# Two small query blocks of the first layer's attention share one round: 16 steps of differential attention become 12

## Chip, cores and metric

One core of a Trainium2 chip runs the kernel. The metric is the device time of one execution in microseconds (us). All times below come from one profiled execution or from the timed runs.

## What is computed

Two transformer blocks in a row over 512 tokens of width 1024, batch 1. The change lies in the attention of the very first layer: 4 heads of differential attention, each with two score maps of head width 64 and values of width 128, in query blocks of 128 with causal key prefixes:

```python
s = jnp.einsum('bqhmd,bkhmd->bhmqk', qi, kf) * scale + bias      # m = 0, 1; bias: ALiBi, causal
p = jax.nn.softmax(s, axis=-1)
attn = p[:, :, 0] - lam * p[:, :, 1]
return jnp.einsum('bhqk,bkhe->bqhe', attn, vf)                   # then an RMS norm per head
```

Beside it in the same layer stands a pooling mixer of 4 groups, and both results go through an output projection. Then come a convolutional gated feed-forward part, a sliding-window layer with its own feed-forward part, and the second block.

## The kernel before

**Weights.** Every large product is made in float32 accuracy from halves: `hi` (ScalarE rounds the loaded weights `raw` to `w_hi`), `lo` (VectorE subtracts, `w_lo = raw - w_hi`), and three products of 512 columns each (hi*hi, hi*lo, lo*hi). Weights come in slabs of 2048 columns through two alternating halves of `raw`, `w_hi` and `w_lo`. Slab s may be rounded once slab s-2 is used up, and used once its `lo` is complete (`lo_done`).

**Stage A.** Slabs 0 to 4 are plain. Slabs 5 to 7 (`A_MORE`, 144 products) and the first two slabs of the output projection, 8 and 9 (`A_OUT`, 96 products), are woven in small portions between the steps of the attention, so that TensorE has work while the softmax goes over the other engines. `A_FILL` cuts these 240 products into portions, one for each step. Products form units that end in one PSUM bank: 24 products for a unit of slabs 5 to 7, 12 for one of slabs 8 and 9. Units take turns in two banks, so that one begins only when the unit before the last has been read (`unit_read`).

**Step g** of the attention, before the change, is head g // 4 and query block g % 4 (key width 128, 256, 384 or 512). Each engine has its own hand-written queue, in program order:

- TensorE: `scores(g)` (2 matmuls, banks 4 and 5), `fill(g)` (a portion of `A_FILL`), `turn(g-1)` (transposes of the finished probabilities into bank 6), then jobs of other chains (`norm_job`: sums of squares for the norms of q and k; `pool_product`; `turn_v`: transposes of a head's values; `squares_summed`: sums of squares over a head's output), then `values(g-2)`.
- VectorE: `finish(g-1)` (reciprocal of the row sums, scaling, difference of the two maps), `maxima(g)` (bias, negation and row minimum), then `scaled`, `output`, `pooled_low`, `sub_scale`, the reading of finished units (`evacuate`), `lo_piece` (the `lo` of a slab, of slabs 8 and later in two halves one step apart), `alibi`, `pool_group`.
- ScalarE: norms and copies of the other chains, `exps(g)`, `copy(g-1)` (the transposed probabilities to SBUF), `hi_piece` (the `hi` of the slab after one that begins in this step).
- GpSimd, in one order over the heads: squares of q and k; then for each of heads 0 to 2 the square of its output (after `output`) and the `lo` half of its normed output (after ScalarE's `sub_split`).
- SyncE: one load for each slab, slab s behind `lo_done` of slab s-2.

Of the kernel before, what the change touches and what calls it, by code (L numbers as in the profile page):

```python
# [112 lines left out]
X_ROUNDS = [(0, 1), (2,), (3,)]  # L113
X_STEPS = 8 * len(X_ROUNDS)
# [48 lines left out]
def blocks_program(nc, weights, xt, params, consts, scratch, out):  # L163
    with ExitStack() as ctx:
# [183 lines left out]
        def f_blocks(r):  # L348

            out, col = [], 0  # L350
            for i in X_ROUNDS[r % 3]:
                out.append((i, col, (i + 1) * P))
                col += (i + 1) * P
            return out

        def f_width(r):
            return sum(w for _, _, w in f_blocks(r))

        def f_done(r):

            return 2 * (4 * (r // 3) + (0, 2, 3)[r % 3])
# [52 lines left out]

        def a_width(g):
            return (g % 4 + 1) * P
# [292 lines left out]
        def _(pe):  # L709
# [106 lines left out]
            def a_stage():  # L816
# [54 lines left out]
                def scores(g):  # L871
                    it, i = g // 4, g % 4
                    if i == 0:
                        pe.wait_ge(d_qk, 2 * it + 2)
                    if g:
                        pe.wait_ge(d_max, 2 * g)
                    for m in range(2):
                        h = 64 * m
                        pe.matmul(psum[:, 4 + m, 0:a_width(g)], qn[it % 2][h:h + 64, i * P:(i + 1) * P], kn[it % 2][h:h + 64, 0:a_width(g)],  # L879
                                  start=True, stop=True).then_inc(d_scored, 1)  # L880

                def turn(g):
                    pe.wait_ge(d_fin, g + 1)
                    if g:
                        pe.wait_ge(d_copied, g)
                    for j in range(g % 4 + 1):
                        last = pe.transpose(psum[:, 6, j * P:(j + 1) * P], a_prob(0, g)[:, j * P:(j + 1) * P], ident)
                    last.then_inc(d_pt, 1)

                def values(g):  # L890
                    it, i = g // 4, g % 4
                    if i == 0:
# [3 lines left out]
                    pe.wait_ge(d_copied, g + 1)  # L896
                    for j in range(i + 1):
                        last = pe.matmul(psum[:, 0, i * P:(i + 1) * P], vtok[it % 2][:, j * P:(j + 1) * P],
                                         a_slot(g)[:, j * P:(j + 1) * P],
                                         start=(i == 0), stop=(i == 3 and j == 3), skip_group_check=True)  # L900
                    last.then_inc(d_pv, 1)
# [25 lines left out]
                for g in range(A_STEPS + 2):  # L927
                    it = g // 4
                    if g < A_STEPS:
                        scores(g)  # L930
                    fill(g)
                    if 1 <= g <= A_STEPS:
                        turn(g - 1)
                    if g % 4 < 2 and it + 1 < A_HEADS:
                        norm_job(2 * (it + 1) + g % 4, 1)
                    if g in (2, 3, 5, 6):
                        pool_product((2, 3, 5, 6).index(g))
                    if g == 1:
                        turn_v(1)
                    elif g in (9, 10):  # L940
                        turn_v(g - 7)
                    elif g % 4 == 3 and it:
                        squares_summed(it - 1)
                    if g >= 2:
                        values(g - 2)
                fill(A_STEPS + 2)
                squares_summed(A_HEADS - 1)
                fill(A_STEPS + 3)
# [145 lines left out]
            def x_stage():  # L1094
                so, xo = FIRST["S_OUT"], FIRST["X_OUT"]

                def mask(r):

                    if r:
                        pe.wait_ge(f_max, f_done(r))  # L1100
                    for m in range(2):
                        for i, col, w in f_blocks(r):
# [3 lines left out]
                def scores(r):  # L1106
# [3 lines left out]
                    for i, col, w in f_blocks(r):  # L1110
                        for m in range(2):
# [3 lines left out]
                            if i == X_ROUNDS[r % 3][-1]:  # L1115
                                last.then_inc(f_scored, 1)

                def turn(r):
                    for m in range(2):
# [3 lines left out]
                        for j in range(f_width(r) // P):  # L1123
# [3 lines left out]
                def values(r):  # L1127
# [6 lines left out]
                    for i, col, w in f_blocks(r):  # L1134
# [201 lines left out]
        def _(act):  # L1336
# [101 lines left out]
            def a_stage():  # L1438
# [15 lines left out]
                def v_copy(it):  # L1454

                    act.wait_ge(d_turned_v, it + 1)
                    if it >= 2:
                        act.wait_ge(d_pv, 4 * (it - 1))
# [27 lines left out]
                def exps(g):  # L1486
                    w = a_width(g)
                    for m in range(2):
                        n = 2 * (g % 4) + m
                        act.wait_ge(d_max, 2 * g + m + 1)  # L1490
                        pr = a_prob(m, g)[:, 0:w]
                        act.activation(pr, pr, ACT.Exp, scale=-1.0, bias=neg_max[:, n:n + 1],
                                       accum_out=row_sum[:, n:n + 1]).then_inc(d_exp, 1)

                def copy(g):
                    w = a_width(g)
                    act.wait_ge(d_pt, g + 1)
                    if g >= 2:
                        act.wait_ge(d_pv, g - 1)
                    act.activation(a_slot(g)[:, 0:w], psum[:, 6, 0:w], ACT.Identity).then_inc(d_copied, 1)  # L1500
# [12 lines left out]
                for g in range(A_STEPS + 2):  # L1513
                    it = g // 4
                    if g % 4 in (1, 2) and it + 1 < A_HEADS:
                        norm_job(2 * (it + 1) + g % 4 - 1, 1)
                    if g in (3, 4, 6, 7):
                        pooled_high((3, 4, 6, 7).index(g))
                    if g == 2:
                        v_copy(1)  # L1520
                    elif g in (10, 11):
                        v_copy(g - 8)
                    elif g % 4 == 0 and it >= 2:
                        sub_norm(it - 2)
                    elif g % 4 == 1 and it >= 2:
                        sub_split(it - 2)
                    if g < A_STEPS:
                        exps(g)
                    if 1 <= g <= A_STEPS:
                        copy(g - 1)  # L1530
                    for s in A_FILL[1][g]:
                        hi_piece(s + 1, 0, 1)
                act.wait_ge(d_pv, A_STEPS)
# [228 lines left out]
            def x_stage():  # L1762
                so, xo = FIRST["S_OUT"], FIRST["X_OUT"]

                def exps(r):
                    n = f_done(r)
                    for m in range(2):
                        for i, col, w in f_blocks(r):
# [6 lines left out]
                def copy(r):  # L1775
                    w = f_width(r)
# [80 lines left out]
        def _(dve):  # L1857
# [93 lines left out]
            def a_stage():  # L1951
# [45 lines left out]
                def maxima(g):  # L1997
                    it, w = g // 4, a_width(g)
                    if g % 4 == 0:
                        me.wait()  # L2000
                    if g >= 2:
                        dve.wait_ge(d_pt, g - 1)
                    for m in range(2):
                        n = 2 * (g % 4) + m
                        dve.wait_ge(d_scored, 2 * g + m + 1)
                        dve.tensor_tensor_reduce(
# [788 lines left out]
```

## Time and profile before

| | us |
|---|---|
| Median of 3 runs | 1901.89 (1901.38 to 1901.93) |
| The profiled execution | 1901.86 |
| Its span, first to last instruction | 1900.0 |
| TensorE busy (share of the span) | 1881.6 (99%) |
| VectorE busy | 1176.5 (62%) |
| ScalarE busy | 789.6 (42%) |
| GpSimd busy | 138.5 (7%) |

The table is read against the 1.9 us by which the execution is longer than its span. The busy shares are those of the whole program; the attention of stage A runs from about 68 to 161 us of it.

### The profile page before, as it was taken

Reading aid. Unit: us, or ns where it says so; the run is one execution under the profiler, and the core shown is the slowest. Engines: PE = TensorE matmul, PEld = TensorE weight load, DVE = VectorE, ACT = ScalarE, POOL = GpSimd, SP = SyncE. Lnnn points to the kernel's source line nnn. Section 1 sums busy time; section 2 is a strip of 40 time slices with the busy share of each in tenths; the row PEclk is TensorE's granted clock in tenths of the full one; section 3 lists DMA queues with packets and bytes.
Section 4 is the critical chain, followed back from the end, with each engine's and each line's share of the span. In section 5 each row is a group of like instructions: output and inputs, shape, how many; then the busy total and the mean of one; then the engine's idle time right before and its main releaser. Section 6 shows DMA issues by size and latency. Waiting matters only on the chain.

```text
span 1900.0 us, 24418 instructions
## 1 busy us (share of the span) xinstructions
PE 1881.6 (99%) x9034; PEld 1504.0 (79%) x9034; DVE 1176.5 (62%) x1826; ACT 789.6 (42%) x1184; POOL 138.5 (7%) x102
## 2 busy tenths in 40 slices
PE   8999999999999999999999999999999999999999
PEld 6767888888887788888888887878777788888887
DVE  5786677356646866763566498665656666744762
ACT  4365443133435654432334343422566544322441
POOL 2012100000021110000000101111211020000000
PEclk9999999999999999999999999999999999999999
DMA  6112222322231122223232322444433122233222
GB/s 216 67 58 72 93 88 88 111 89 102 71 106 65 46 89 89 88 88 111 89 102 76 121 89 91 144 149 156 134 128 112 49 96 100 77 100 111 89 78 99
DMA packets 38304, 186.51 MB, mean 98 GB/s; under 512 B 4384, under 2 KB 4768, under 8 KB 23376
## 3 DMA queue, kind: packets, MB, share of 16 engines
q1 hardware_dynamic: 37936, 185.22, 28.8%
q8 instruction: 49, 0.80, 0.2%
q10 hardware_dynamic: 288, 0.23, 0.0%
q14 instruction: 31, 0.25, 0.0%
HBM read 176.95 MB, written 8.49 MB: 98 GB/s over the span
## 4 chain that ended last, share of the span: by engine, by line
PE 92%; DVE 5%; ACT 2%; DMA 1%; issue 1%; SPq 0%; DVEq 0%; ACTq 0%
PE banks L723 55%; PE banks L1199 22%; PE banks L773 4%; PE banks L1113 1%; PE banks L1138 1%; DVE w_lo L1869 1%; PE banks L1124 1%; PE banks L1272 1%; PE banks L1243 1%; PE banks L1084 1%; DVE tmp L2255 1%; PE banks L1255 1%; PE banks L1212 1%; ACT w_hi L1352 1%; DMA raw<-weights 1%; PE banks L879 1%
## 5 line engine op out<-in xcount | busy, mean ns | idle before, releaser
L723 PE MATMUL banks<-xn_hi,w_hi 128*128 128x512 f32 x1240 | 486.5, 392 | 6.4 <-DVE w_lo L2632 6.4
L723 PE MATMUL banks<-xn_hi,w_lo 128*128 128x512 f32 x1240 | 483.6, 390 | 0.0
L723 PE MATMUL banks<-xn_lo,w_hi 128*128 128x512 f32 x1240 | 478.1, 390 | 0.0
L1352 ACT ACTIVATE w_hi<-raw 128x2048 fp32r<-128x2048 f32 (+2 forms) x134 | 228.3, 1704 | 230.6 <-PE banks L723 194.2
L1869 DVE TENSOR_TENSOR w_lo<-raw,w_hi 128x2048 fp32r<-128x2048 f32 (+2 forms) x134 | 274.9, 2051 | 46.0 <-ACT w_hi L1352 45.6
L723 PEld LDWEIGHTS banks<-xn_hi,w_hi 128*128 128x128 f32 x1240 | 233.6, 188 | 57.6 <-DMA con<-consts 6.3
L723 PEld LDWEIGHTS banks<-xn_lo,w_hi 128*128 128x128 f32 x1240 | 233.4, 188 | 49.5 <-issue 1.4
L723 PEld LDWEIGHTS banks<-xn_hi,w_lo 128*128 128x128 f32 x1240 | 233.5, 188 | 48.6
L1414 ACT ACTIVATE tmp<-scaled_h,par 128x512 f32<-128x512 f32 x132 | 100.6, 809 | 349.2 <-DVE scaled_h L1914 349.1
L1914 DVE TENSOR_TENSOR scaled_h<-banks,token_rs 128x512 f32<-128x512 f32 x132 | 85.1, 686 | 184.9 <-PE banks L723 164.7
L1199 PE MATMUL banks<-xn_hi,w_hi 128*128 128x512 f32 x408 | 165.6, 406 | 1.0 <-DVE big L1964 0.6
L1199 PE MATMUL banks<-xn_lo,w_hi 128*128 128x512 f32 x408 | 162.4, 398 | 0.0
L1199 PE MATMUL banks<-xn_hi,w_lo 128*128 128x512 f32 x408 | 162.1, 397 | 0.0
L723 PE MATMUL banks<-hid_hi,w_hi 128*128 128x512 f32 x396 | 154.0, 389 | 0.0
L723 PE MATMUL banks<-hid_lo,w_hi 128*128 128x512 f32 x396 | 154.0, 389 | 0.0
L723 PE MATMUL banks<-hid_hi,w_lo 128*128 128x512 f32 x396 | 154.0, 389 | 0.0
L1887 DVE TENSOR_TENSOR x<-banks,x 128x512 f32<-128x512 f32 (+1 forms) x48 | 33.2, 692 | 178.4 <-PE banks L723 157.2
L638 POOL TENSOR_TENSOR sq<-sq 128x512 f32<-128x512 f32 x38 | 59.2, 1558 | 858.0 <-ACT sq L1358 837.4
L1922 DVE SCALAR_TENSOR_TENSOR tmp<-scaled_h,par,tmp 128x511 f32<-128x511 f32 x132 | 98.8, 748 | 34.9 <-ACT tmp L1414 34.9
L1926 DVE SCALAR_TENSOR_TENSOR tmp<-scaled_h,par,tmp 128x510 f32<-128x510 f32 x132 | 99.1, 750 | 15.1 <-DVE tmp L1922 13.0
L2122 DVE TENSOR_TENSOR w_lo<-raw,w_hi 128x1024 fp32r<-128x1024 f32 (+1 forms) x61 | 82.4, 1355 | 40.6 <-ACT w_hi L1554 40.6
L1199 PEld LDWEIGHTS banks<-xn_hi,w_hi 128*128 128x128 f32 x408 | 76.6, 188 | 30.6 <-issue 13.1
(270 smaller groups left out, 2564.3 us busy)
## 6 DMA issues: line engine op xcount, KB each, us to landing
raw<-weights SPq DMA_DIRECT2D x116, 1024.0 KB, 4.9
raw<-weights SPq DMA_DIRECT2D x24, 768.0 KB, 4.3
raw<-weights SPq DMA_DIRECT2D x24, 640.0 KB, 3.9
big<-scratch SPq DMA_DIRECT2D x40, 256.0 KB, 4.6
att<-scratch SPq DMA_DIRECT2D x16, 256.0 KB, 4.6
scratch<-stage SPq DMA_DIRECT2D x12, 256.0 KB, 4.3
scratch<-con SPq DMA_DIRECT2D x12, 256.0 KB, 2.0
out<-x SPq DMA_DIRECT2D x4, 512.0 KB, 4.0
```

Source lines behind the costliest of these rows:

```text
L638: pool.tensor_tensor(chunk(sq, 0), chunk(sq, 0), chunk(sq, c), ALU.add).then_inc(sq_summed, 1)
L723: return pe.matmul(psum[:, 2 * p + m, :], w[:, at_:at_ + P], x_part(k), start=start, stop=stop)
L773: return pe.matmul(psum[:, 2 * (s % 2), :], w[:, at_:at_ + P], x_part(k), start=(k == 0 and t == 0), stop=(k == k_n - 1 and t == 2))
L1199: ins = pe.matmul(c_bank(u), w[:, at_:at_ + P], x_part(k), start=(k == 0 and t == 0), stop=(k == k_n - 1 and t == 2))
L1352: act.activation(w_hi[:, sl], raw[:, sl], ACT.Identity).then_inc(hi_done, 1)
L1414: act.activation(chunk(tmp, 2 * j + m), chunk(scaled_h, 2 * j + m), ACT.Identity, bias=pcol(conv_b, c), scale=pcol(conv, 3 * c + 2)).then_ ...
L1869: dve.tensor_tensor(w_lo[:, sl], raw[:, sl], w_hi[:, sl].bitcast(F32), ALU.subtract).then_inc(lo_done, 1)
L1887: last = dve.tensor_tensor(chunk(x, c), psum[:, 2 * ((a + j) % 2) + m, :], chunk(x, c), ALU.add)
L1914: dve.tensor_tensor(chunk(scaled_h, 2 * j + m), psum[:, 2 * ((a + j) % 2) + m, :], token_rs[:, :], ALU.mult).then_inc(h_scaled, 1)
L1922: me.mark(dve.scalar_tensor_tensor(out=chunk(tmp, t, 1), in0=bank[:, 0:T - 1], scalar=pcol(conv, 3 * c + 1), in1=chunk(tmp, t, 1), op0=ALU ...
L1926: dve.scalar_tensor_tensor(out=chunk(tmp, t, 2), in0=bank[:, 0:T - 2], scalar=pcol(conv, 3 * c), in1=chunk(tmp, t, 2), op0=ALU.mult, op1=A ...
L2122: ins = dve.tensor_tensor(w_lo[:, sl], raw[:, sl], w_hi[:, sl].bitcast(F32), ALU.subtract)
```

## The change

Query blocks 0 and 1 of a head share a round: their scores lie side by side in the two score banks (128 and 256 columns of 512), and so do their transposes in bank 6. Blocks 2 and 3 have a round each. A head has three rounds instead of four steps, all heads 12 instead of 16. All matmuls, transposes, exponentials, minima and scalings stay as many and as wide as they were. Only the reciprocal, the copy of the transposes and the waits go by round.

The 240 woven products are cut anew, and the jobs of the other chains get new places in the order. The functions that name the blocks of a round exist already for the second block's attention; they get neutral names and serve both.

```diff
-A_STEPS = 4 * A_HEADS
-A_FILL = weave([("A_MORE", 3), ("A_OUT", 2)], [20] * 4 + [16] + [12] * 4 + [7] * 8 + [8] + [12, 20])
+BLOCK_ROUNDS = [(0, 1), (2,), (3,)]
+A_ROUNDS = len(BLOCK_ROUNDS) * A_HEADS
+A_FILL = weave([("A_MORE", 3), ("A_OUT", 2)], [24] * 6 + [12] * 3 + [8, 8, 4] + [4, 4] + [12, 20])
...
+                    for i, col, w in round_blocks(r):
+                        for m in range(2):
+                            h = 64 * m
+                            last = pe.matmul(psum[:, 4 + m, col:col + w], qn[it % 2][h:h + 64, i * P:(i + 1) * P], kn[it % 2][h:h + 64, 0:w],
+                                             start=(col == 0), stop=True, skip_group_check=True)
+                            if i == BLOCK_ROUNDS[r % 3][-1]:
+                                last.then_inc(d_scored, 1)
...
+                for r in range(A_ROUNDS + 2):
+                    it = r // 3
+                    if r < A_ROUNDS:
+                        scores(r)
+                    fill(r)
+                    if 1 <= r <= A_ROUNDS:
+                        turn(r - 1)
+                    if r % 3 < 2 and it + 1 < A_HEADS:
+                        norm_job(2 * (it + 1) + r % 3, 1)
+                    if r == 0:
                         turn_v(1)
...
+                    elif r == 2:
+                        pool_product(0)
+                        pool_product(1)
+                    elif r == 3:
+                        pool_product(2)
+                    elif r == 5:
+                        pool_product(3)
+                    elif r in (7, 8):
+                        turn_v(r - 5)
+                    elif r in (6, 9, 11):
+                        squares_summed((6, 9, 11).index(r))
+                    if r >= 2:
+                        values(r - 2)
...
+                for r in range(A_ROUNDS + 2):
+                    it = r // 3
+                    if r in (7, 10, 12):
+                        sub_norm((7, 10, 12).index(r))
+                    if r in (1, 8, 9):
+                        v_copy((1, 8, 9).index(r) + 1)
+                    if r % 3 and it + 1 < A_HEADS:
+                        norm_job(2 * (it + 1) + r % 3 - 1, 1)
...
+                    if r in (8, 11, 13):
+                        sub_split((8, 11, 13).index(r))
+                    if r < A_ROUNDS:
+                        exps(r)
+                    if 1 <= r <= A_ROUNDS:
+                        copy(r - 1)
+                    for s in A_FILL[1][r]:
                         hi_piece(s + 1, 0, 1)
...
+                for r in range(A_ROUNDS + 2):
+                    it = r // 3
+                    if 1 <= r <= A_ROUNDS:
+                        finish(r - 1)
+                    if r < A_ROUNDS:
+                        maxima(r)
+                    if r % 3 and it + 1 < A_HEADS:
+                        scaled(2 * (it + 1) + r % 3 - 1)
+                    if r % 3 == 2 and 1 <= it < A_HEADS:
                         output(it - 1)
...
+                    if r == 3:
+                        pooled_low(0)
+                        pooled_low(1)
+                    elif r in (4, 6):
+                        pooled_low(2 if r == 4 else 3)
+                    if r in (7, 10, 12):
+                        h = (7, 10, 12).index(r)
+                        sub_scale(h, chunk(big, h))
+                    if r:
+                        for s, m in A_FILL[2][r - 1]:
                             evacuate(s, m)
                     for q in range(2):
...
+                        if r > q:
+                            for s in A_FILL[1][r - q - 1]:
                                 if s + 1 >= o:
                                     lo_piece(s + 1, q, 2)
```

Read from the list of portions: slabs 5, 6 and 7 begin in rounds 0, 2 and 4, slab 8 in round 6, slab 9 in the middle of round 10. `A_FILL[1][r]` is the list of slabs that begin in round r, `A_FILL[2][r]` that of the units that end in it. The last two portions, behind the last `values`, are 12 and 20 products as before.

## Rows read from the trace of the kernel before

**Rows 1.** The page: busy time by engine, and the chain that ended last.
```profile
PE 1881.6 (99%) x9034; PEld 1504.0 (79%) x9034; DVE 1176.5 (62%) x1826; ACT 789.6 (42%) x1184; POOL 138.5 (7%) x102
...
PE 92%; DVE 5%; ACT 2%; DMA 1%; issue 1%; SPq 0%; DVEq 0%; ACTq 0%
```

**Rows 2.** Timeline of TensorE: start, duration, line, tiles, shape; L879 scores, L898 values.
```profile
67.83 0.49 PE L879 MATMUL banks<-att 64*128 64x128 f32 x4
...
88.11 0.38 PE L898 MATMUL banks<-att 128*128 128x128 f32 x2
88.43 1.13 PE L879 MATMUL banks<-att 64*128 64x512 f32 x4
...
95.48 0.61 PE L898 MATMUL banks<-att 128*128 128x128 f32 x4
96.02 0.49 PE L879 MATMUL banks<-att 64*128 64x128 f32 x4
...
101.50 0.83 PE L898 MATMUL banks<-att 128*128 128x128 f32 x6
102.26 0.70 PE L879 MATMUL banks<-att 64*128 64x256 f32 x4
102.89 0.50 PE L1199 MATMUL banks<-xn_hi,w_hi 128*128 128x512 f32 x1
```

**Rows 3.** Windows, each from a portion's first product to the next piece's start.
```profile
68.25:72.92 4.67, 4.67 (x23) 3.87 (x22) 4.50 (x13) 2.69 (x5) 0.00 (x0) 1.00 0.00 0
125.24:126.97 1.73, 1.73 (x9) 1.38 (x8) 1.52 (x5) 1.73 (x6) 0.91 (x1) 1.00 0.01 5
133.97:136.59 2.62, 1.89 (x9) 1.23 (x8) 2.51 (x7) 0.00 (x0) 0.00 (x0) 1.00 0.00 0
138.79:141.19 2.40, 1.90 (x10) 1.24 (x8) 2.29 (x6) 1.50 (x3) 0.00 (x0) 1.00 0.39 58
150.15:152.81 2.66, 1.96 (x9) 1.31 (x8) 2.29 (x7) 1.52 (x4) 0.00 (x0) 1.00 0.00 0
157.10:159.41 2.31, 2.20 (x12) 1.51 (x11) 2.31 (x4) 0.94 (x2) 0.95 (x1) 1.00 0.00 0
160.21:163.35 3.14, 3.13 (x15) 2.27 (x14) 2.74 (x3) 0.60 (x1) 0.37 (x1) 1.00 0.28 42
```

**Rows 4.** Timeline of TensorE: a wait before a product of step 2.
```profile
84.20 0.47 PE L1199 MATMUL banks<-xn_hi,w_hi 128*128 128x512 f32 x1 [0.56 <-DVE big L1964]
```

**Rows 5.** Timeline of VectorE: L2006 minima, L2030 pooled_low, L1964 unit read, L2122 lo.
```profile
89.70 0.69 DVE L2006 CUSTOM_DVE_ANT_0 att<-banks,att 128x512 f32<-128x512 f32 x1 [3.48 <-PE banks L879]
...
96.68 0.29 DVE L2006 CUSTOM_DVE_ANT_0 att<-banks,att 128x128 f32<-128x128 f32 x1 [0.58 <-PE banks L879]
...
116.87 0.75 DVE L2030 SCALAR_TENSOR_TENSOR big_r<-banks,par,big_r 128x512 fp32r<-128x512 f32 x1
117.54 0.68 DVE L1964 TENSOR_TENSOR big<-banks,token_rs 128x512 f32<-128x512 f32 x1
118.14 1.22 DVE L2122 TENSOR_TENSOR w_lo<-raw,w_hi 128x1024 fp32r<-128x1024 f32 x1
...
132.65 2.06 DVE L2122 TENSOR_TENSOR w_lo<-raw,w_hi 128x1024 fp32r<-128x1024 f32 x1
```

**Rows 6.** Timeline of ScalarE: hi of a slab, and sub_split.
```profile
153.73 1.90 ACT L1554 ACTIVATE w_hi<-raw 128x2048 fp32r<-128x2048 f32 x1
...
157.75 0.63 ACT L1484 ACTIVATE big_r<-big 128x512 fp32r<-128x512 f32 x1 [0.33 <-DVE big L2036]
```

**Rows 7.** Timeline of GpSimd: L659 lo of a head's output, L657 its square.
```profile
126.06 1.29 POOL L659 TENSOR_TENSOR big_r<-big,big_r 128x512 fp32r<-128x512 f32 x1 [13.23 <-ACT big_r L1484]
132.15 1.48 POOL L657 TENSOR_TENSOR tn<-big 128x512 f32<-128x512 f32 x1 [4.80 <-DVE big L2025]
...
148.68 1.04 POOL L657 TENSOR_TENSOR tn<-big 128x512 f32<-128x512 f32 x1 [4.05 <-DVE big L2025]
```

**Rows 8.** A window at the start of the kernel.
```profile
6.00:12.00 6.00, 5.64 (x13) 4.46 (x14) 3.62 (x7) 4.20 (x8) 0.00 (x0) 1.00 1.03 370
```

More of the change, by code:

```diff
@@ L354, in f_blocks, with round_width, blocks_done @@
             return out
-        def f_width(r):
-            return sum(w for _, _, w in f_blocks(r))
-        def f_done(r):
+        def round_width(r):
+            return sum(w for _, _, w in round_blocks(r))
+        def blocks_done(r):
             return 2 * (4 * (r // 3) + (0, 2, 3)[r % 3])
@@ L895, in values @@
                             pe.wait_ge(d_out, it)
[L896 to L900, printed above, removed]
+                    pe.wait_ge(d_copied, r + 1)
+                    for i, col, w in round_blocks(r):
+                        for j in range(i + 1):
+                            last = pe.matmul(psum[:, 0, i * P:(i + 1) * P], vtok[it % 2][:, j * P:(j + 1) * P],
+                                             a_slot(r)[:, col + j * P:col + (j + 1) * P],
+                                             start=(i == 0), stop=(i == 3 and j == 3), skip_group_check=True)
                     last.then_inc(d_pv, 1)
@@ L926, in a_stage @@
                 pe.wait_ge(banks_read, 4)
[L927 to L938, printed above, removed]
-                        turn_v(1)
[L940 to L946, printed above, removed]
+                for r in range(A_ROUNDS + 2):
[8 more added lines that the diff above has]
+                    if r == 0:
+                        turn_v(1)
+                    elif r == 2:
[11 more added lines that the diff above has]
+                        values(r - 2)
+                fill(A_ROUNDS + 2)
                 squares_summed(A_HEADS - 1)
-                fill(A_STEPS + 3)
+                fill(A_ROUNDS + 3)
                 for s in (FIRST["A_OUT"] + 2, FIRST["A_OUT"] + 3):
@@ L1109, in scores @@
                         pe.wait_ge(f_qk, 2 * it + 2)
-                    for i, col, w in f_blocks(r):
+                    for i, col, w in round_blocks(r):
                         for m in range(2):
@@ L1512, in a_stage @@
                 hi(5, 0)
[L1513 to L1531, printed above, removed]
+                for r in range(A_ROUNDS + 2):
+                    it = r // 3
+                    if r in (7, 10, 12):
[5 more added lines that the diff above has]
+                    if r == 3:
+                        pooled_high(0)
+                        pooled_high(1)
+                    elif r in (4, 6):
+                        pooled_high(2 if r == 4 else 3)
+                    if r in (8, 11, 13):
[5 more added lines that the diff above has]
+                    for s in A_FILL[1][r]:
                         hi_piece(s + 1, 0, 1)
-                act.wait_ge(d_pv, A_STEPS)
+                act.wait_ge(d_pv, A_ROUNDS)
                 act.wait_ge(sub_stat, A_HEADS - 1)
@@ L2019, in finish @@
                     me.wait()
-                    dve.scalar_tensor_tensor(out=p0, in0=p0, scalar=row_inv[:, n:n + 1], in1=p1,
-                                             op0=ALU.mult, op1=ALU.add).then_inc(d_fin, 1)
+                    for i, col, w in blocks:
+                        n = 2 * i
+                        p0, p1 = a_prob(0, r)[:, col:col + w], a_prob(1, r)[:, col:col + w]
+                        last = dve.scalar_tensor_tensor(out=p0, in0=p0, scalar=row_inv[:, n:n + 1], in1=p1, op0=ALU.mult, op1=ALU.add)
```

165 lines of the change are left out of this document (75 added, 90 removed).

## The prediction

> **What bounds the kernel now.** I read the page first. TensorE is busy 99% of the span and makes up 92% of the chain that ended last [rows 1]. So only two things can shorten this kernel: less work on TensorE, or less waiting of TensorE. What the softmax engines save by themselves is worth nothing.
>
> Then I read TensorE's timeline of the attention stage piece by piece, to get a price for each piece and to see where it stood still. A wait that is shorter than a matmul's modelled end hides in the busy time, so I take waits from start to start: a portion of 20 products takes 4.67 and one of 7 takes 1.73 [rows 3]. That makes 0.226 for a product and 0.15 for going from the scores into a portion. By this price three portions of 7 should take 1.73 and took 2.62, 2.40 and 2.66; one of 8 should take 1.96 and took 2.31; one of 12 should take 2.86 and took 3.14 [rows 3]. The waits are 0.89 + 0.67 + 0.93 + 0.35 + 0.28 = 3.1, and with the 0.56 in step 2 [rows 4] 3.7. The idle before a row counts from a modelled end, so the last one is a little more: 3.7 to 4.2, of which I take **4.0 us of waits** in the stage. Two kinds are among them: VectorE's `finish` is late for `turn` (the first two), and a unit's bank is read late (the others).
>
> The matmuls themselves stay the same in number and width, so 4.0 us plus the small cost of passing between pieces is all that the change can win: about 0.26% of the kernel.
>
> **The change part by part.**
>
> *Fewer groups on TensorE.* Four portions fewer to enter: 4 x 0.15 = 0.60. The scores of blocks 0 and 1 cost 0.42 (67.83 to 68.25) and 0.63 (102.26 to 102.89) [rows 2, 3], together 1.05 as before. `values` costs 0.32 for one matmul, 0.54 for two and 0.76 for three [rows 2]: three in one go instead of one and two save 0.10 a head, 0.40 in all. One `norm_job` now stands directly ahead of scores where two pieces did before; by the same kind of passage I put 0.1 against it. Gain: **0.9 us**, between 0.6 and 1.0.
>
> *The old waits.* In rounds 0 to 5 each portion is a whole unit of 24 products, 24 x 0.226 + 0.15 = 5.6 us, and a unit's bank has a full round to be read. The 0.56 goes. In the later rounds a `finish` is due after a longer round (8 to 12 products and the longer jobs, instead of 7), and the unit of products 192 to 203 ends two rounds ahead of the reader that needs its bank. I let all 4.0 us go; between 3.7 and 4.2 if they all do. What may stay is a term of its own below.
>
> *VectorE and ScalarE.* Four reciprocals and four copies fewer, as many minima, exponentials and scalings. Both engines are off the path, so this is nothing by itself. What counts is the order.
>
> *A new wait at round 6: the second half of slab 8's `lo`.* Slab 7 begins in round 4. So `hi` of slab 8 is made in ScalarE's round 4, and VectorE makes the first half of its `lo` in round 5 and the second half in round 6. But TensorE's portion of round 6 begins with slab 8 and waits for the whole `lo`. On VectorE that half stands behind `maxima(6)`, which needs `scores(6)`, which TensorE issues directly ahead of the portion. Counted from the start of `scores(6)`:
> - Minima can start about 1.2 later. For one block the distance was 1.27 at 512 columns (88.43 to 89.70) and 0.66 at 128 (96.02 to 96.68) [rows 2, 5]. For two blocks the first map is ready only with the third matmul, 0.42 + 0.32 after the start, plus a tail of 0.45 to 0.74 (0.66 less the 0.21, 1.27 less the 0.53 that the first matmul takes): 1.2 to 1.5.
> - Four minima, two of 128 and two of 256 columns. The rows are 0.29 and 0.69 long, of which the last 0.08 overlaps what follows [rows 5]: 0.21 at 128, 0.61 at 512, so some 0.35 at 256: 1.12.
> - `pooled_low(3)` 0.67, the reading of the unit that ended in round 5, 0.60, and the half slab, 1.22 (116.87, 117.54, 118.14) [rows 5].
>
> The sum is 1.2 + 1.12 + 0.67 + 0.60 + 1.22 = 4.8; `scores(6)` itself covers 1.05. TensorE stands for **3.8 us**. The half slab took 2.06 where GpSimd worked beside it [rows 5, 7]; here GpSimd has nothing to do (the square of head 0's output is long made, and its next job waits for `sub_split`), so I take 1.22. With 2.06 the wait is 4.6; with some of the minima's start overlapped, 3.4. Behind the waiting product on TensorE are `turn(5)`, two jobs of the norms, `values(4)` and `scores(7)`: the whole stage moves, and nothing hides this. Before the change the same half stood three steps ahead of its use. SyncE's load of slab 10 waits for this `lo` too, but is needed only four rounds later.
>
> *A new wait at round 11: the square of head 2's output.* `squares_summed(2)` and the `output(2)` that it rests on are now in the same round. Two chains lead to it on GpSimd; the later one decides. Counted from the start of `scores(11)`, TensorE arrives after 1.06 + (4 x 0.226 + 0.15) + 0.33 (`turn(10)`, three transposes at 0.11) = 2.44.
> - By VectorE: minima 1.27 to 2.5, `output(2)` to 3.1, square of 1.04 to 1.48 [rows 7]: 4.2 to 4.6.
> - By ScalarE: `hi_piece(10)` comes in ScalarE's round 10, since slab 9 begins there, and `sub_split(1)` comes first in round 11, behind it. `copy(9)` ends some 0.4 ahead of `scores(11)`, `hi_piece(10)` adds 1.8 (row of 1.90) and `sub_split(1)` 0.6 (row of 0.63) [rows 6]: 2.05. GpSimd, in program order, first makes the `lo` half of head 1's output, 1.29, then the square, 1.04 [rows 7]: 4.4 at least, 4.9 with a square of 1.48 beside VectorE's half slab.
>
> So the wait is 2.0 to 2.5, and up to 3.2 if `exps(10)` holds ScalarE longer. I take **2.5 us**. Behind it on TensorE are `values(9)`, the last two small portions and `values(10)` and `values(11)`: only 8 products remain to cover anything.
>
> *Small lateness elsewhere.* `finish(8)` has half a slab of `lo` and `alibi` ahead of it, and at `turn(8)` it is about as late as TensorE is; `turn(11)` is near too. 0.2, between 0 and 1.0 (about one wait as before the change).
>
> **Sum.** -4.0 - 0.9 + 3.8 + 2.5 + 0.2 = +1.6 us. On the profiled execution's 1901.86 that gives 1903.5; that execution is within 0.03 of the median, so the median should be 1903.5 as well. The tail behind `values(11)` has the same portions and the same chain, so nothing more moves there. With all bounds on one side: -4.2 - 1.0 + 3.4 + 2.0 = +0.2 and -3.7 - 0.6 + 4.6 + 3.2 + 1.0 = +4.5: 1902.1 to 1906.4.
>
> **The rivals.** A change under 0.2% (3.8 us: below 1898.1 or above 1905.7 it counts) is what measurement here can't tell from none.
>
> *A slower clock after the long wait (other side: slower).* The granted clock is 1.00 through the stage, the 2.4 GHz level, and the longest waits in it are near 0.9 us [rows 3]. At the start of the kernel the array ran at half pace: 13 products in 6 us [rows 8], where 20 take 4.67 [rows 3], though the column of the granted clock says 1.00 there as well. It had done nothing for 6.36 us before. If the 3.8 us of idleness in round 6 bring that pace back for as long, it costs half of 5.6, 2.8 us: 1906.3. It decides if the clock drops at all. For it: this would be four times the longest wait of the stage. Against it: it is shorter than the idleness at the start, and one wait is all. The Trainium skill, "TensorE: Matmul & The Clock Gate", Part 1 on the HAM clock gate, says that an idle array goes back to half the clock and that only sustained activity lifts it again; by that rule the outcome would be this rival's 1906.3, and no run so far shows which side of it such a wait falls on. Chance 0.13.
>
> *VectorE stays late for `turn`.* The two first waits of [rows 3] are of this kind, 0.8 each. If three such waits remain in rounds 8 to 11, where portions shrink to 8 and 4, it is +2.4: 1905.9. For it: rounds 10 and 11 carry few products. Against it: TensorE's standing in round 6 lets VectorE and ScalarE catch up, and every round holds longer jobs than the old steps. Chance 0.12.
>
> *The new waits are not there.* If VectorE's half slab comes in time, for instance because scores and minima run ahead further than I read, 3.8 go: 1899.7, and without the second wait too 1897.2. Against it: the order of the queues leaves no way, `maxima(6)` needs `scores(6)`. Chance 0.06.
>
> **How the numbers follow.** My forecast (both waits, clock holds) has 0.69. Its own range is 1902.1 to 1906.4, mostly below 1905. The range of 1901.0 to 1906.2 leaves out the third rival and most of the first, with thin tails of the forecast: about 2 in 10. Within 0.2%: 0.64 of the forecast's 0.69, 0.06 and 0.03 of the first two rivals and 0.04 of the third, 0.77. Slower: 0.05 + 0.07 + 0.09 less rounding, 0.20. Faster: only if both new waits are missing, 0.03.
>
> **What would show it.** In the profile after: a wait of TensorE of some 3.8 us ahead of the first product of slab 8, released by L2122's `lo`, around 120 us; one of 2 to 3 us ahead of the head's squares, released by GpSimd, around 153; no waits for `finish` above 0.3; portions of 24 in 5.6. Products after the long wait 0.23 apart say that the clock held, 0.43 apart that it fell. The prediction is wrong if TensorE comes to slab 8 with the `lo` made, or if waits of another place sum to over 1 us.

## The result and the profile after

The changed kernel takes 1904.88 us (median of 20 runs, 1903.68 to 1905.99), the kernel before 1901.41 in as many runs beside it (1900.83 to 1901.93). The ratio is 1.0017, 95% interval 1.0011 to 1.0024: slower by 3.5 us, by less than the 0.2% that I had set as the bound. The forecast was +1.6 us (1903.5), in a range that holds the result. The two new waits that it named are there, at their place and nearly at their price. The clock, which I had expected to hold, did not.

The profiled execution took 1905.70 with a span of 1903.9. First the page of the changed kernel, part 1 and the chain:

```profile
PE 1881.8 (99%) x9034; PEld 1505.7 (79%) x9034; DVE 1174.0 (62%) x1822; ACT 788.0 (41%) x1180; POOL 139.8 (7%) x102
...
PE 92%; DVE 5%; ACT 2%; issue 1%; DMA 1%; SPq 0%; POOL 0%; DVEq 0%; ACTq 0%; POOLq 0%
```

It says as little as before [rows 1]. TensorE's timeline tells more (L877 scores, L887 `turn`, L866 `squares_summed`, L899 `values`, L1205 woven products):

```profile
68.21 0.93 PE L877 MATMUL banks<-att 64*128 64x128 f32 x8
...
119.76 0.93 PE L877 MATMUL banks<-att 64*128 64x128 f32 x8
124.51 1.22 PE L1205 MATMUL banks<-big_r,w_hi 128*128 128x512 f32 x2 [3.82 <-DVE w_lo L2143]
...
154.79 0.49 PE L887 MATMUL banks<-con,att 128*128 128x128 f32 x3
157.37 1.30 PE L866 MATMUL banks<-tn,con 128*128 128x512 f32 x2 [2.09 <-POOL tn L654]
158.46 1.49 PE L899 MATMUL banks<-att 128*128 128x128 f32 x6
```

Nothing stands between 68 and 119 us, where the kernel before had waited in step 2 [rows 4]. Then come the two waits that the prediction named: for the second half of slab 8's `lo` in round 6, and for GpSimd's square in round 11. VectorE's timeline in round 6 shows the queue that the first one hangs on (L2015 minima, L2047 `pooled_low`, L1972 the reading of a unit, L2143 `lo`):

```profile
120.86 0.29 DVE L2015 CUSTOM_DVE_ANT_0 att<-banks,att 128x128 f32<-128x128 f32 x1 [1.60 <-PE banks L877]
...
121.98 0.75 DVE L2047 SCALAR_TENSOR_TENSOR big_r<-banks,par,big_r 128x512 fp32r<-128x512 f32 x1
122.64 0.68 DVE L1972 TENSOR_TENSOR big<-banks,token_rs 128x512 f32<-128x512 f32 x1
123.24 1.22 DVE L2143 TENSOR_TENSOR w_lo<-raw,w_hi 128x1024 fp32r<-128x1024 f32 x1
```

From `scores(6)` at 119.76: minima 1.10 later, 1.12 long, then 0.66, 0.60 and 1.22. That is 4.70, where 4.8 was forecast.

For the second wait, these are rows of ScalarE (`hi` of slab 10, `sub_split(1)`), of GpSimd (the `lo` of head 1's output, the square of head 2's) and of VectorE (`output(2)`):

```profile
152.55 1.90 ACT L1562 ACTIVATE w_hi<-raw 128x2048 fp32r<-128x2048 f32 x1
154.36 0.62 ACT L1490 ACTIVATE big_r<-big 128x512 fp32r<-128x512 f32 x1
```
```profile
155.05 1.27 POOL L656 TENSOR_TENSOR big_r<-big,big_r 128x512 fp32r<-128x512 f32 x1 [11.76 <-ACT big_r L1490]
156.28 1.03 POOL L654 TENSOR_TENSOR tn<-big 128x512 f32<-128x512 f32 x1
```
```profile
155.20 0.69 DVE L2042 COPY big<-banks 128x512 f32<-128x512 f32 x1
```

`output(2)` is done at 155.89, and GpSimd could take the square only at 156.28, behind the `lo`. The chain by ScalarE decides, as forecast.

What was not forecast is behind the waits. Windows of the changed kernel (length, busy time of PE, PEld, DVE, ACT, POOL, then the granted clock as a share of 2.4 GHz, DMA share, GB/s):

```profile
119.76:124.51 4.75, 0.93 (x10) 0.53 (x9) 3.65 (x12) 1.99 (x9) 0.00 (x0) 0.95 0.00 0
124.51:128.74 4.23, 4.23 (x12) 3.35 (x13) 1.66 (x7) 0.00 (x0) 0.00 (x0) 0.65 0.72 248
...
157.37:161.45 4.08, 4.08 (x12) 2.98 (x13) 3.85 (x7) 1.32 (x2) 0.00 (x0) 0.60 0.01 2
157.37:158.00 0.63, 0.63 (x2) 0.39 (x3) 0.63 (x1) 0.00 (x0) 0.00 (x0) 1.00 0.00 0
...
132.50:135.40 2.90, 2.90 (x14) 2.32 (x13) 1.86 (x6) 2.69 (x6) 0.00 (x0) 1.00 0.01 3
...
124.51:126.50 1.99, 1.99 (x5) 1.61 (x6) 1.66 (x7) 0.00 (x0) 0.00 (x0) 0.50 0.52 99
```

The portion of 12 in round 6 took 4.23 us where the same portion in round 7 took 2.90: for its first 2 us the granted clock was 0.50, the 1.2 GHz level. After the second wait the same: `squares_summed(2)`, `values(9)` and the portion of 4 took 4.08 us at 0.60, where their prices at full clock are 0.86 + 0.60 + 1.03 = 2.5 (2.72 behind such a wait, as a run below shows). TensorE had done nothing for 3.9 us ahead of the first slow stretch and for 2.25 us ahead of the second, which began only some 0.6 us after the standstill.

From `scores(0)` to `squares_summed(3)` (68.21 to 167.19) the stage takes 98.98 us. Before, it took 95.52 (67.83 to 163.35) [rows 2, 3]. That is +3.46, the whole difference of the medians. I use this length of the stage below: it is free of what happens at the start of the kernel, where executions differ by some 1.0 us (`scores(0)` starts between 67.16 and 68.21 in the traces).

### The profile page after: what moved, and what is told of

Read it like the earlier page. It is cut to its first block, busy times and chain, and to the rows that moved or that the text cites. A ratio compares the mean times of both kernels' runs of the same rounds, so it can differ in the third digit from the quotient of the medians.

```text
span 1903.9 us, 24403 instructions
## 1 busy us (share of the span) xinstructions
PE 1881.8 (99%) x9034; PEld 1505.7 (79%) x9034; DVE 1174.0 (62%) x1822; ACT 788.0 (41%) x1180; POOL 139.8 (7%) x102
## 4 chain that ended last, share of the span: by engine, by line
PE 92%; DVE 5%; ACT 2%; issue 1%; DMA 1%; SPq 0%; POOL 0%; DVEq 0%; ACTq 0%; POOLq 0%
PE banks L720 55%; PE banks L1205 22%; PE banks L770 4%; PE banks L1119 1%; PE banks L1144 1%; DVE w_lo L1877 1%; PE banks L1130 1%; PE banks L1278 1%; PE banks L1249 1%; PE banks L1090 1%; DVE tmp L2276 1%; PE banks L1261 1%; PE banks L1218 1%; ACT w_hi L1358 1%; DMA raw<-weights 1%
## 5 line engine op out<-in xcount | busy, mean ns | idle before, releaser
L1205 PE MATMUL banks<-xn_hi,w_hi 128*128 128x512 f32 x408 | 165.5, 406 | 0.5 <-DVE w_lo L2143 0.5
L1205 PE MATMUL banks<-xn_lo,w_hi 128*128 128x512 f32 x408 | 162.3, 398 | 0.0
L1205 PE MATMUL banks<-xn_hi,w_lo 128*128 128x512 f32 x408 | 161.8, 397 | 0.0
L2143 DVE TENSOR_TENSOR w_lo<-raw,w_hi 128x1024 fp32r<-128x1024 f32 (+1 forms) x61 | 82.0, 1347 | 40.7 <-ACT w_hi L1562 40.7
L1205 PEld LDWEIGHTS banks<-xn_hi,w_hi 128*128 128x128 f32 x408 | 76.6, 188 | 30.1 <-issue 13.0
```

Of the source, the lines that this page charges most:

```text
L1205: ins = pe.matmul(c_bank(u), w[:, at_:at_ + P], x_part(k), start=(k == 0 and t == 0), stop=(k == k_n - 1 and t == 2))
L2143: ins = dve.tensor_tensor(w_lo[:, sl], raw[:, sl], w_hi[:, sl].bitcast(F32), ALU.subtract)
```

## The experiments

In all of them the stage is read from `scores(0)` to `squares_summed(3)`. Ratios are to the kernel before, in runs beside it on the same chip.

### Both causes taken away, singly and together

Slab 8's `lo` as a whole in VectorE's round 5:

```diff
-                                if s + 1 >= o:
+                                if s + 1 > o:
                                     lo_piece(s + 1, q, 2)
```

> The changed kernel with both halves of slab 8's lo made in VectorE's round 5 (as one piece) instead of one half in round 5 and one in round 6. Theory of the order (the half in round 6 makes TensorE stand for 3.9 us, and the array is slow for a while after it, 1.5 us): the idle ahead of slab 8's first product goes, its 12 products take 2.9 instead of 4.2 us, and the median falls from 1904.9 by some 5.4 to about 1899.5. Rival (VectorE is short of time and the wait only moves): finish is late for turn in rounds 6 to 10, waits of 2 us or more appear there and the median stays at 1901.5 or above.

Measured: 1898.84 us, ratio 0.9985 (0.9976 to 0.9994); stage 93.83. The wait ahead of slab 8 is gone, its portion takes 2.96, and the waits for `finish` that the rival wanted are not there. What is left of the stage's waits, apart from 0.2 at `turn(8)`, in that kernel's timeline of TensorE:

```profile
152.09 2.08 PE L866 MATMUL banks<-tn,con 128*128 128x512 f32 x2 [2.11 <-POOL tn L654]
```

and its windows of that wait and of what follows:

```profile
149.80:152.09 2.29, 0.18 (x3) 0.01 (x1) 2.29 (x5) 1.67 (x5) 2.23 (x2) 0.98 0.00 0
152.09:155.09 3.00, 3.00 (x8) 1.97 (x9) 2.55 (x5) 0.80 (x2) 0.00 (x0) 0.50 0.00 0
```

The gain against the changed kernel is 6.0 us by the medians (0.32% by the ratios), a little more than the 5.4 expected.

`squares_summed(2)` a round later, with what follows it:

```diff
-                    elif r in (6, 9, 11):
-                        squares_summed((6, 9, 11).index(r))
+                    elif r in (6, 9, 12):
+                        squares_summed((6, 9, 12).index(r))
...
-                    if r in (7, 10, 12):
-                        sub_norm((7, 10, 12).index(r))
+                    if r in (7, 10, 13):
+                        sub_norm((7, 10, 13).index(r))
```

(and `sub_scale(2)` in round 13 likewise).

> The changed kernel with squares_summed(2) in TensorE's round 12 instead of 11, sub_norm(2) and sub_scale(2) in round 13 instead of 12. Theory of the order (2.25 us of waiting for GpSimd's square and about 1.5 us of slow array after it, both in rounds 11 and 12): both go, the long wait in round 6 stays, median about 1901.2. Rival (ScalarE and VectorE are late at this place whatever TensorE asks for first): turn(11) or values waits instead, and the median stays above 1903.5.

> Both moves together. Theory of the order: the gains add, -5.4 and -3.7, median about 1895.8, granted clock 1.000 as before the change. Rival (standing in round 6 lets VectorE and ScalarE catch up, so without it they are late for turn in rounds 8 to 11): 1898 or above.

Measured: 1905.14, ratio 1.0020 (1.0011 to 1.0029), stage 98.67, so the later square alone wins nothing. Both moves together: 1900.55, ratio 0.9993 (0.9984 to 1.0002), stage 93.30, no better than the first alone. Both forecasts failed. The rival of the second run came true, and that of the third by its time, though its waits lie in rounds 11 and 12 and not in 8 to 11. The timeline of TensorE in the second kernel shows where the wait went:

```profile
155.62 0.91 PE L899 MATMUL banks<-att 128*128 128x128 f32 x6 [0.70 <-issue]
...
159.75 0.66 PE L887 MATMUL banks<-con,att 128*128 128x128 f32 x4 [2.29 <-DVE att L2037]
```

`values(9)` comes too early for `output(2)`, whose copy empties its bank (VectorE had it from 154.84 to 155.53), and `turn(11)` too early for `finish(11)`. VectorE's timeline says why `finish(11)` is late:

```profile
156.04 2.03 DVE L2143 TENSOR_TENSOR w_lo<-raw,w_hi 128x1024 fp32r<-128x1024 f32 x1
157.99 0.15 DVE L2023 RECIPROCAL small<-small 128x2 f32<-128x2 f32 x1
...
158.95 0.75 DVE L2037 SCALAR_TENSOR_TENSOR att<-att,small 128x512 f32<-128x512 f32 x1
```

Half of slab 10's `lo` stands ahead of it, 0.8 us longer than the 1.22 that the same instruction takes at 159.62, while GpSimd squares head 2's output beside it (155.94 to 156.99). So the square was only the last of several chains that end in rounds 11 and 12, where 8 products cover all of them.

### The price of the clock

The first wait left in place, and 14 products with no use put into it, in a bank that nobody reads until it is written anew:

```diff
+                    if r == 6:
+                        pe.wait_ge(pool_low, 3)
+                        for _ in range(14):
+                            pe.matmul(psum[:, 7, :], xn_hi[:, 0:P], xh(0), start=True, stop=True)
                     fill(r)
```

> The changed kernel with 14 additional products of 512 columns between scores(6) and the portion of slab 8, into bank 7, which nobody reads until it is written anew; they take 3.2 us and lie inside the wait of 3.9 us. The wait itself stays. Theory that the idleness lowers the array's clock: the 12 products behind it take 2.9 instead of 4.2 us and the median falls by about 1.4 to 1903.5. Rival (the slow products after the wait have another cause, such as the operands of slab 8): they still take 4.2 us and the median stays at 1904.9 or rises.

Measured: 1903.53, ratio 1.0009 (1.0000 to 1.0018), stage 96.22. Its windows of the wait and of the portion behind it:

```profile
119.85:123.73 3.88, 3.46 (x16) 2.55 (x14) 3.64 (x12) 1.87 (x8) 0.00 (x0) 1.00 0.00 0
123.73:126.59 2.86, 2.86 (x12) 2.31 (x13) 1.67 (x7) 0.00 (x0) 0.00 (x0) 1.00 0.59 206
...
152.97:155.22 2.25, 0.16 (x2) 0.00 (x0) 2.25 (x5) 1.63 (x5) 2.20 (x2) 1.00 0.00 0
155.22:157.94 2.72, 2.72 (x13) 1.73 (x13) 2.61 (x6) 1.32 (x2) 0.00 (x0) 1.00 0.00 0
```

Slab 8's first product comes as late as before, but the portion takes 2.86 instead of 4.23 at a granted clock of 1.00. The kernel does more work and is 1.4 us faster. The intervals of the two ratios overlap, so the windows carry this and the times agree with it.

The last two rows are the second wait, which this kernel still has, and the three pieces behind it. It is as long as in the changed kernel, 2.25 us, but in this execution the clock stayed at 1.00, and the pieces took 2.72 instead of 4.08. So the stage is shorter by 2.8 us here, 1.4 from each wait, and only the first 1.4 is the work of the 14 products.

The same for the second wait, in the kernel with the whole `lo` in round 5: 9 products ahead of `squares_summed(2)`.

> The changed kernel with all of slab 8's lo in round 5, and with 9 additional products of 512 columns ahead of squares_summed(2), inside its wait of 2.1 us. Theory that the wait also slows the array: squares_summed(2) takes 0.86 instead of 1.86 us and values(9) 0.6 instead of 1.1, median 1.5 below that of the same kernel without the products, 1897.3. Rival (2.1 us of idleness seldom lowers the clock): median about 1898.8.

Measured: 1898.47, ratio 0.9984 (0.9975 to 0.9993), stage 92.43. The median moved by 0.4, not 1.5, and the single runs tell why. Time and mean granted clock of each run, sorted:

```
without: 1897.47 1.000  1898.23 1.000  1898.61 1.000  1898.70 1.000  1898.77 1.000  1898.84 0.999
         1898.87 1.000  1899.92 0.999  1899.97 0.999  1900.20 0.999  1900.44 0.999
with:    1897.99 to 1899.28, 1.000 in all eleven
```

Without the products, the four slowest of the eleven runs have a lowered clock and lie 1 to 1.5 us above the next (a fifth run with 0.999 doesn't); with them there are none. In the profiled execution without them (one of the four) the 1.4 us between the two stages is the slow stretch (3.00 at 0.50 there, in the rows above). So a wait of 2.3 us lowers the clock in some executions only. The mean clock of a run is a rough sign of it: the profiled executions of the last cut and of the graded portions with `output(2)` late, both below, show a mean of 0.999 and yet a granted clock of 1.00 in every stretch of 2 us. In the changed kernel all 20 runs show 0.998 or 0.999, and the six with 0.999 are the fastest: 1903.68 to 1904.20 against 1904.42 to 1905.99. Its wide spread, 2.3 us against 1.1 before, goes with the clock.

### Order alone, then portions

The changed kernel's portions, all of `lo` 8 in round 5, `output(2)` ahead of `maxima(11)`, and `sub_split(1)` ahead of `hi` of slab 10:

```diff
+                    if r == 11:
+                        output(2)
                     if r < A_ROUNDS:
                         maxima(r)
...
                         copy(r - 1)
+                    if r == 10:
+                        sub_split(1)
                     for s in A_FILL[1][r]:
                         hi_piece(s + 1, 0, 1)
```

> The changed kernel's own portions with three moves in the order: all of slab 8's lo in round 5, output(2) ahead of maxima(11), sub_split(1) ahead of hi of slab 10. Theory: no wait ahead of slab 8 or of squares_summed(2), but turn(11) waits about 2 us for finish(11), since rounds 11 and 12 hold 4 products each and hi and lo of slab 10 stand ahead of exps(11) and finish(11): median about 1897.0. Rival (that last chain is short enough): no wait, median 1895.

Measured: 1898.57, ratio 0.9984 (0.9975 to 0.9993), stage 92.53. I had expected one wait of 2 us at `turn(11)`. There are two: 1.17 ahead of `squares_summed(2)` and 0.75 ahead of `turn(11)`, and the median is 1.6 us above the 1897.0 expected. The first is new of its kind. GpSimd's and VectorE's timelines of this kernel (L656 the `lo` of head 1's output, L2039 the last instruction of `finish(10)`, L2044 `output(2)`):

```profile
147.81 1.28 POOL L656 TENSOR_TENSOR big_r<-big,big_r 128x512 fp32r<-128x512 f32 x1 [9.96 <-ACT big_r L1490]
```
```profile
147.78 1.73 DVE L2039 SCALAR_TENSOR_TENSOR att<-att,small 128x384 f32<-128x384 f32 x1
149.43 0.68 DVE L2044 COPY big<-banks 128x512 f32<-128x512 f32 x1
```

With `sub_split(1)` earlier, GpSimd's `lo` of head 1's output falls on the last instruction of `finish(10)`, which takes 1.73 instead of the 0.62 of the changed kernel (at 153.21, GpSimd idle), and `output(2)`, the square and `squares_summed(2)` are late by as much. The Trainium skill, "SBUF — State Buffer", section "SBUF: two separate sides", says that VectorE and GpSimd share one pair of ports that one of them holds for a whole instruction. The trace agrees: 1.1 us is lost beside an instruction of 1.28, and VectorE's ends 0.42 us after GpSimd's. In the graded kernel below, where it began 0.24 us after GpSimd's (147.40 against 147.16) and not 0.03 before it, it takes 1.53 and ends 0.41 after, as far as GpSimd's spans can be read so finely.

Now the portions. First with a round more between slabs and their use, but with portions of 22 that are no whole units:

```diff
-[24] * 6 + [12] * 3 + [8, 8, 4] + [4, 4] + [12, 20]
+[22] * 6 + [12] * 4 + [10, 10] + [4, 4] + [12, 20]
```

> The changed kernel with portions of 22 (six rounds), 12 (four), 10, 10, 4, 4, 12, 20, and output(2) ahead of maxima(11) on VectorE. Slab 8 then begins in round 7 and slab 9 in round 11, so that slab 8's lo is complete a round ahead of its use, and hi of slab 10 comes behind exps(11) instead of ahead of sub_split(1). Theory (the waits come from places in the order and from too few products in rounds 11 and 12, and each long wait costs slow products too): no wait above 0.7 us in the stage, granted clock 1.000 in every run, about 5.4 us faster than before the change, median 1896.3. Rival (fewer rounds leave VectorE and ScalarE too little time, whatever the order): waits of 2 us or more remain and the median is 1899 or above.

> The same portions, with output(2) where the change has it, behind maxima(11). Theory: in round 11 squares_summed(2) waits about 0.4 to 1 us for output(2) and the square behind it, median about 1896.8. Rival (the second wait of the changed kernel came by ScalarE alone): no difference from the kernel with output(2) moved.

Measured: 1906.18 (ratio 1.0028, 1.0019 to 1.0037), stage 100.28, and 1905.46 (ratio 1.0021, 1.0012 to 1.0030), stage 98.08. Both forecasts failed; by their medians they are the slowest kernels of the study. The timeline of TensorE of the first:

```profile
86.05 0.47 PE L1205 MATMUL banks<-xn_hi,w_hi 128*128 128x512 f32 x1 [1.74 <-DVE big L1972]
...
97.33 0.50 PE L1205 MATMUL banks<-xn_hi,w_hi 128*128 128x512 f32 x1 [1.75 <-DVE big L1972]
...
108.17 0.47 PE L1205 MATMUL banks<-xn_hi,w_hi 128*128 128x512 f32 x1 [1.19 <-DVE big L1972]
...
118.12 0.50 PE L1205 MATMUL banks<-xn_hi,w_hi 128*128 128x512 f32 x1 [0.88 <-DVE big L1972]
```

Units of 24 in portions of 22 end early in a portion; the unit that begins there needs a bank that VectorE reads only in this round, behind `finish` and `maxima`: 5.6 us in four rounds. I had counted the rounds for slabs, and for units only from slab 8 on. This is the old wait of step 2 [rows 4] in each of the rounds 2 to 5, and it goes in the changed kernel because its portions of 24 are whole units. The rest of the loss came late: a wait for a bank ahead of the portion of round 13, 1.86 of idle, was followed by a lowered clock:

```profile
161.47:164.25 2.78, 2.78 (x13) 2.54 (x13) 2.78 (x3) 0.00 (x0) 2.12 (x1) 0.63 0.00 0
```

Which of the two forms of `output(2)` is better can't be read from this pair: the profiled executions differ in the clock, and the single runs spread over 4 to 6 us.

Then portions that keep whole units where that matters and give rounds 11 and 12 more products, with `lo` 8 in round 5 and `output(2)` ahead:

```diff
-[24] * 6 + [12] * 3 + [8, 8, 4] + [4, 4] + [12, 20]
+[24] * 6 + [12] + [8] * 6 + [4] + [12, 20]               # eights
+[24] * 6 + [12, 12, 10, 8, 6, 6, 6, 4] + [12, 20]        # graded
+[24] * 6 + [12] * 3 + [6, 6, 8, 8, 4] + [8, 20]          # last cut
```

> The changed kernel with all of slab 8's lo in round 5, output(2) ahead of maxima(11), and the portions behind round 6 cut as 8, 8, 8, 8, 8, 8, 4 instead of 12, 12, 8, 8, 4, 4, 4; the first six stay whole units of 24. Slab 9 begins in round 11, so hi of slab 10 comes behind exps(11). Theory (a portion may straddle a unit's end only where the unit before the last was read a round earlier; rounds 11 and 12 need about 6 products each to cover the last softmax): no wait in rounds 10 to 12 above 1 us, but rounds 7 and 8 are short for VectorE (6.9 us of work in round 8 against 4.5 of TensorE), so turn(8) waits 1.5 to 2.5 us: median 1897.5 to 1898.5. Rival (VectorE's order has slack enough there): 1896.

> The same with the portions behind round 6 cut as 12, 10, 8, 6, 6, 6, 4. Theory: rounds 7 and 8 cover VectorE, rounds 11 and 12 the last softmax; what stays is about 0.5 at turn(8) and 0.7 at squares_summed(2), since GpSimd's lo of head 1's output meets finish(10) on VectorE. Median 1896.8, the fastest of all, clock 1.000 in every run. Rival (as with portions of 22, the new cuts bring waits for banks): 1899 or above.

> The portions of the one before, with output(2) behind maxima(11) as in the changed kernel. Theory (output(2) sets the square where hi of slab 10 no longer does): squares_summed(2) waits about 1.9 us instead of 0.7, median 1.2 above the one before, 1898.0, and some runs lose another 1.4 to a slower array. Rival (GpSimd's own queue sets it): no difference.

> The graded kernel (all of slab 8's lo in round 5, output(2) ahead of maxima(11)) with portions of six times 24, then 12, 12, 12, 6, 6, 8, 8, 4, and 8 instead of 12 behind the last values: four products come from behind the attention into rounds 11 and 12. Theory (each 2 products there cover 0.45 us of the wait ahead of squares_summed(2), 1.2 before, and the square of the last output needs fewer than 8 products of cover): waits of the stage fall from some 2.0 to 1.2 us, median 1897.5. Rival (the unit that begins within the portion of 8 waits for its bank, or the square of the last head's output is late): 1898.3 or above.

| | median | ratio, interval | stage |
|---|---|---|---|
| eights | 1899.40 | 0.9988 (0.9979 to 0.9997) | 93.26 |
| graded | 1898.26 | 0.9982 (0.9973 to 0.9991) | 92.11 |
| graded, `output(2)` late | 1900.85 | 0.9996 (0.9987 to 1.0005) | 93.30 |
| last cut | 1897.64 | 0.9978 (0.9969 to 0.9987) | 91.59 |

The first three are slower than forecast by 0.9 to 2.9 us, the last as forecast (1897.5). The eights were to lose at `turn(8)`, and lose elsewhere: 0.7 ahead of `values(6)`, which needs `output(1)` to empty its bank, 0.6 for GpSimd's square, and 1.24 for a bank in round 13. `output(2)` matters: behind `maxima(11)` the square costs 2.39 us of waiting against 1.17, and the stage is 1.2 us longer, as forecast. The medians are 2.6 us apart. The other 1.4 would fit a slow stretch behind the longer wait, and ten of the eleven runs have a mean clock of 0.999 against two, but it isn't shown: the profiled execution is the fastest of its eleven, and its clock stayed up:

```profile
149.49:152.10 2.61, 0.22 (x3) 0.00 (x1) 2.54 (x9) 2.35 (x6) 1.04 (x1) 1.00 0.00 0
152.10:155.12 3.02, 3.02 (x15) 2.24 (x16) 1.37 (x3) 2.54 (x3) 0.00 (x0) 1.00 0.00 0
```

The last cut has the lowest median of the study (its interval overlaps that of the graded portions), 4.1 us faster than the kernel before and 0.39% below the changed one. Its timeline of TensorE holds the two waits that remain (in the stage, idle of 0.3 us and more):

```profile
141.06 0.66 PE L887 MATMUL banks<-con,att 128*128 128x128 f32 x4 [0.48 <-DVE att L2037]
...
151.33 1.12 PE L866 MATMUL banks<-tn,con 128*128 128x512 f32 x2 [1.00 <-POOL tn L654]
```

## Why the prediction came out as it did

Each term of the sum, forecast and as read from the two timelines:

- **Old waits that go**: -4.0 forecast, -4.1 measured (3.1 by the windows [rows 3], 0.8 in step 2 from start to start, 0.1 at two `turn`s). All went; none of them is between 68 and 119 us or in the portions of rounds 7 and 10, which take their price (2.90 for 12, 1.97 for 8).
- **Fewer groups**: -0.9 forecast, about -1.7 measured. The four portions less and `values` are as priced. Mis-sized was the step "the scores of blocks 0 and 1 cost 0.42 and 0.63, together 1.05 as before". Four matmuls in one go take 0.86 (68.21 to 69.07, the portion's first product), as two of 384 columns do (0.85). So 0.19 of each passage was a fixed cost of the group, four times.
- **Wait at round 6**: +3.8 forecast, +3.9 measured (scores end 0.86 after 119.76, product at 124.51). Place and queue as forecast; the queue was 0.1 shorter than the 4.8 forecast, and the scores covered 0.86 of it and not 1.05. Before the change the half slab was made two steps ahead of its use (118.14 [rows 5], used at 125.24 [rows 3]), not three as the prediction has it; the sum doesn't rest on this. Shown by the run with all of `lo` 8 in round 5.
- **Wait at round 11**: +2.5 forecast, +2.25 measured (155.12, three transposes at 0.11 after 154.79, to 157.37). The deciding chain was the forecast one, ScalarE's `hi` of slab 10, `sub_split(1)` and GpSimd's two jobs. What was not seen is that other chains end in the same rounds only 1 to 2 us sooner.
- **Small lateness**: +0.2 forecast, +0.2 measured: the portion ahead of `turn(8)` and the wait behind it take 2.14 instead of 1.96.
- **Clock**: 0 forecast, +2.7 measured: 4.23 - 2.86 = 1.4 behind the first wait, 4.08 - 2.72 = 1.4 behind the second. This is the step that failed: "my forecast (both waits, clock holds)". The rival that I gave 0.13 came true, and also where I had not looked for it, behind a wait of 2.25 us. Its size was taken wrongly too, 2.8 for one stretch: the slow stretch behind the first wait lasted some 2.7 us, not 5.6, and cost half of that.
- **Starting again**: not in the forecast, +0.2 measured. Behind the second wait the three pieces took 2.72 and not 2.5 even at a clock of 1.00.

Together -4.1 - 1.7 + 3.9 + 2.25 + 0.2 + 2.7 + 0.2 = +3.45 against +3.46 measured. Two errors of 0.8 and 2.7 us partly cancel, so the time was nearer than the reasons were. That the range holds the result is luck in part: its upper end came from waits that might have been longer, and what filled it was the clock. The sentence of the Trainium skill that I had put beside the rival ("TensorE: Matmul & The Clock Gate", Part 1: an idle array goes back to half the clock) was right here about the clock, which the trace has at 0.50. The 1906.3 that I had put beside it came from a slow stretch of 5.6 us, and the time was 1904.88.

The rival of a VectorE that stays late for `turn` did not happen in the changed kernel. It was covered: as soon as the square no longer waited, `turn(11)` waited 2.29 by its row. The rival without new waits did not happen.

Open: why the clock fell behind the second wait in some executions and not in others. Behind the first, of 3.9 us, it fell in both profiled executions that have it unfilled (the changed kernel and the one with the later square). Seven profiled executions have an unfilled wait of 2.1 to 2.6 us, from the end of TensorE's last piece by its price to the next start. The clock fell behind it in three: 2.25 in the changed kernel, 2.29 with `lo` in round 5, 2.11 with portions of 22. It stayed at 1.00 in four: 2.25 in the kernel with 14 products, 2.46 ahead of `turn(11)` in each of the two with the later square, 2.61 with `output(2)` late. So the length alone doesn't decide it in this span, and no run here varies it by itself.

## What to carry to other kernels

When steps of a pipeline are merged, list for each producer and consumer how many rounds lie between them before and after. Three distances shrank to nothing in these kernels: a weight half behind a minimum that needs the scores just issued, a copy and its square in one round, and, with portions of 22, a unit's bank read in the round that wants it. They cost 3.9, 2.25 and 0.9 to 1.75 us, where merging had saved 1.7 us beside the old waits. When a wait is taken away, ask which chain ends next in the same round: taking away the last alone gave nothing, and giving that round more work shortened the stage by 0.5 us (92.11 to 91.59; the medians are too near to tell). A standstill of TensorE such as the one of 3.9 us is priced at its length plus some 1.4 us of slow array; at 2.1 to 2.6 us the 1.4 came in some executions only.

## What was not expected of the hardware

- A standstill of 2.1 to 2.3 us was enough in some executions to lower the granted clock to 0.50, and one of 3.9 us did it in both profiled executions; yet one of 2.6 us left it at 1.00. The slow stretch costs 1.4 us each. 14 useless products inside the wait kept it at 1.00 and made the kernel faster.
- Four score matmuls in one group (two of 128 and two of 256 columns, on two halves of the rows) took 0.86 us, as groups of 0.42 and 0.63 before: each group has about 0.2 us that does not depend on its columns.
- An instruction of VectorE with two inputs in SBUF took 1.73 instead of 0.62 us beside one of GpSimd of 1.28; one that reads PSUM was not lengthened (0.68 for the minima at 150.03 beside the square at 150.19; 0.69 at 153.97 in the changed kernel, with GpSimd idle).
